# Moving the top-k selection earlier beside the projections, and adding the second softmax map on TensorE, in a two-layer hybrid block

## The chip, the cores and the metric

The kernel runs on 1 core of one Trainium2 chip. One core has TensorE (PE), which multiplies matrices out of SBUF into eight PSUM banks, and VectorE (DVE), ScalarE (ACT) and GpSimd (POOL), which work on tiles of 128 partitions; SyncE (SP) issues the transfers between HBM and SBUF. The metric is the device time of one execution of the whole program, in microseconds (us), lower is better.

## The reference, cut to what matters

The program computes two transformer blocks on a sequence of 1024 tokens of width 1024, batch 1, all in float32. The change lies in the first block's mixer alone: the input projection, the index branch and the two kinds of attention.

```python
h = x @ w_in                       # queries, keys, values of all branches
out_a = gmlp_mixer(a_u, a_v, ...)  # u * (spatial weights @ layer_norm(v))

# differential attention, 4 heads, 2 maps each, 128-query blocks i = 0..7
logits = q[h, m] @ k[h, m].T * scale - slope[h] * |t - s|     (masked)
attn   = softmax(logits[m=0]) - lam * softmax(logits[m=1])
o      = attn @ v[h]               # then rms_norm over the 128 values

# attention on selected keys, 4 heads of 64
score  = sum over 8 index heads of wi * relu(qi @ ki.T)
sel    = the 256 keys of highest score of each query (ties: lowest index first)
p      = softmax(q @ k[sel].T * scale - slope * distance)
o      = p @ v[sel]

x = layer_norm(alpha * x + concat(out_a, out_b, out_c) @ w_out)
```

The feed-forward parts and the second block follow, and the change does not touch them.

## The kernel before, in words

Each engine has a program of its own, written out by hand, and the engines meet only at semaphores. Within an engine the order of instructions is the order in which the Python generators are stepped, so a place where one instruction waits holds back all that stands behind it on that engine.

**Projections.** Weights come in units of 128x1024 float32. SP loads a unit into one of three `raw` buffers, ACT rounds it to the high part `wh` (`act_feed`, L399), POOL subtracts to get the low part `wl` (`pool_feed`, L408), and five such pairs are held. A projection is 24 matmuls (high by high, high by low, low by high). There are 48 projection steps, `s` = 0 to 47: 8 for the gMLP branch ("a", 512 columns wide), 8 for the values of the first attention ("b", 512), 8 for the values of the second ("c", 256), and 24 for queries and keys (two per unit). Their results go through four PSUM banks. For queries and keys ACT writes the high half and `dve_project` (L867) subtracts the low half.

**Beside them.** The list `turns` says how the streams interleave on each of PE, ACT and DVE: 0 is one step of the selection stream, 1 is one projection, 2 is one step of the gMLP's layer norm, 3 is the gMLP product. The selection stream is 20 score units (PE L908, ACT relu L922, DVE sum L934 and L937), then 31 bits, then an end. In a score unit ACT must have emptied the four score banks of the unit before, before PE writes the next.

**The bits.** The 256th highest score of each query is found bit by bit, from the top: for a trial threshold, DVE counts in four of the six query blocks (L964, with the count as a second output), ACT counts in the two widest by summing signs (L956), and small DVE instructions on 6 columns settle the bit and set the next trial. The end is one step that corrects ACT's thresholds by one representable number and counts once more (`dve_next_up`, then L964), and six steps that mark the kept keys of a block (`jk`, a running sum, two comparisons, and the distance bias where a key is kept).

**Attention.** 48 events stand in a fixed order: 8 blocks of head 0 of the first kind ("b"), then b and "c" (second kind, two heads at once) in turn, then 8 b, then b and c in turn. At place `t`, PE runs the logits of event `t` (L1151), the product with the values of event `t - 4` (L1242), and turns the weights of event `t - 2` (L1216, a transpose by the identity). DVE adds the bias and takes the row maximum (L1178), and scales it (L1182). ACT takes the exponential (L1188), copies the turned weights (L1228) and writes the outputs (L1265). For a b event DVE adds the second map to the first (`dve_whole`, L1197, L1199, L1202) before PE turns the sum. On DVE eight places of the attention alternate with the last seven steps of the selection. Logits pass through four banks and the turned weights and outputs through four others.

## Time and profile before

| what | value |
|---|---|
| median of 3 runs | 2943.95 us (2943.65 to 2946.85) |
| the profiled execution | 2947.86 us, of which the span of the core is 2945.7 us |
| busy in the span: PE, DVE, ACT, POOL | 2629.0, 1167.8, 829.2, 622.3 us |
| granted clock of TensorE, mean | 0.945 of full speed |
| first score unit and first projection | from 91.5 us on |
| last projection ends, attention's first logits start | about 396 us |
| last product with values ends | about 657 us |
| the mixed rows are turned for the output projection | from 668.07 us on |

The profile shows one execution. Start times are microseconds from the start of the span. A row of the timeline is one instruction, or several alike merged (xN), with the time from the first's start to the last's end; the bracket says how long the engine had been idle and which instruction released it. Matmuls overlap in the pipeline, so a single matmul lasts longer than the distance from one to the next.

### The profile page before, as it was taken

What the parts mean: (1) busy time and instruction counts of PE and PEld (TensorE: products, weight loads), DVE (VectorE), ACT (ScalarE), POOL (GpSimd) and SP (SyncE); (2) the same over time, 40 slices, a digit from 0 to 9 for tenths busy, and PEclk for the clock granted to TensorE, in tenths of its full rate; (3) what the DMA queues carried; (4) which work ended last, traced back from release to release, by engine and by line L of the source; (5) the groups of instructions that cost most, each with busy time, mean ns of one, the idle gap of its engine ahead of it and who ended that gap; (6) DMA issues with size and microseconds to landing.
All of it is one profiled execution on the core that took longest, in us unless ns stands there. A gap on an engine that the chain in (4) does not pass through costs nothing.

```text
span 2945.7 us, 31283 instructions
## 1 busy us (share of the span) xinstructions
PE 2629.0 (89%) x12551; PEld 2109.2 (72%) x12551; DVE 1167.8 (40%) x2259; ACT 829.2 (28%) x1510; POOL 622.3 (21%) x313
## 2 busy tenths in 40 slices
PE   5999946878898999999994989999859999999998
PEld 4677735767686887887873866666748788788786
DVE  1369998662722323223226015556251111111114
ACT  2345545661311111121112114334231111111022
POOL 1011210001111211221225114447111122222120
PEclk9999978989999999999996999999979999999999
DMA  4013541204023232323411110001231111111122
GB/s 134 22 56 92 181 166 46 84 20 160 8 65 93 86 84 85 97 65 101 129 51 75 47 29 15 15 15 44 72 107 44 43 43 57 48 39 58 36 86 93
DMA packets 195720, 205.45 MB, mean 70 GB/s; under 512 B 13788, under 2 KB 143340, under 8 KB 195576
## 3 DMA queue, kind: packets, MB, share of 16 engines
q1 hardware_dynamic: 195576, 203.46, 21.7%
q8 instruction: 99, 1.62, 0.2%
q14 instruction: 45, 0.37, 0.0%
HBM read 170.88 MB, written 32.56 MB: 69 GB/s over the span
## 4 chain that ended last, share of the span: by engine, by line
PE 71%; DVE 18%; ACT 4%; issue 3%; POOL 2%; DMA 2%; SPq 0%; DVEq 0%; ACTq 0%; POOLq 0%
PE bank L427 12%; PE bank L428 12%; PE bank L429 12%; PE bank L450 8%; PE bank L451 7%; PE bank L452 7%; DVE junk L964 4%; PE bank L1971 2%; PE bank L1242 2%; DVE res L1178 1%; ACT sq L537 1%; PE bank L469 1%; POOL wl L408 1%; PE bank L1151 1%; PE bank L1959 1%
## 5 line engine op out<-in xcount | busy, mean ns | idle before, releaser
L408 POOL TENSOR_TENSOR wl<-raw,wh 128x1024 fp32r<-128x1024 f32 x189 | 452.5, 2412 | 2099.5 <-ACT wh L399 2099.5
L427 PE MATMUL bank<-yh,wh 128*128 128x512 f32 x1536 | 602.1, 392 | 10.1 <-DVE ql L1917 7.2
L429 PE MATMUL bank<-yh,wl 128*128 128x512 f32 x1536 | 598.7, 390 | 0.0
L428 PE MATMUL bank<-yl,wh 128*128 128x512 f32 x1536 | 598.7, 390 | 0.0
L399 ACT ACTIVATE wh<-raw 128x1024 fp32r<-128x1024 f32 x189 | 195.9, 1053 | 613.2 <-PE bank L452 256.3
L427 PEld LDWEIGHTS bank<-yh,wh 128*128 128x128 f32 x1536 | 289.2, 188 | 79.4 <-issue 8.3
L429 PEld LDWEIGHTS bank<-yh,wl 128*128 128x128 f32 x1536 | 288.9, 188 | 60.4
L428 PEld LDWEIGHTS bank<-yl,wh 128*128 128x128 f32 x1536 | 289.1, 188 | 59.5 <-issue 0.2
L1642 DVE TENSOR_TENSOR sil_gate<-sil_gate,bank 128x512 f32<-128x512 f32 x44 | 30.3, 688 | 379.7 <-PE bank L429 379.7
L1662 DVE TENSOR_TENSOR res<-bank,res 128x512 f32<-128x512 f32 x112 | 76.1, 689 | 257.6 <-PE bank L452 257.5
L1642 DVE TENSOR_TENSOR sil_gu<-sil_gu,bank 128x512 f32<-128x512 f32 x44 | 30.3, 688 | 327.0 <-PE bank L429 217.3
L450 PE MATMUL bank<-wh,yh 128*128 128x512 f32 x384 | 154.8, 403 | 2.6 <-DVE yl L2031 1.4
L451 PE MATMUL bank<-wl,yh 128*128 128x512 f32 x384 | 152.4, 397 | 0.0
L452 PE MATMUL bank<-wh,yl 128*128 128x512 f32 x384 | 151.9, 396 | 0.0
L2050 POOL TENSOR_TENSOR took<-took,rest 128x512 f32<-128x512 f32 (+3 forms) x96 | 112.5, 1191 | 89.2 <-DVE rest L2011 50.9
L450 PE MATMUL bank<-wh,hh_gu 128*128 128x512 f32 x256 | 106.9, 418 | 9.0 <-DVE hm_gu L1646 6.7
L964 DVE TENSOR_SCALAR_CACHE_REDUCE junk<-score,cand 128x384 bf16<-128x384 f32 (+3 forms) x132 | 108.9, 825 | 4.7
L450 PE MATMUL bank<-wh,hh_gate 128*128 128x512 f32 x256 | 101.4, 396 | 8.9 <-DVE hm_gate L1646 6.7
L469 PE MATMUL bank<-con,res 128*128 128x128 f32 x192 | 35.3, 342 | 81.5 <-POOL res L1759 31.2
L451 PE MATMUL bank<-wl,hh_gu 128*128 128x512 f32 x256 | 105.1, 410 | 0.0
L452 PE MATMUL bank<-wh,hl_gu 128*128 128x512 f32 x256 | 103.9, 406 | 0.0
L452 PE MATMUL bank<-wh,hl_gate 128*128 128x512 f32 x256 | 100.9, 394 | 0.0
(285 smaller groups left out, 4465.6 us busy)
## 6 DMA issues: line engine op xcount, KB each, us to landing
raw<-in_w_cond SPq DMA_DIRECT2D x48, 512.0 KB, 3.9
raw<-in_w_gu SPq DMA_DIRECT2D x44, 512.0 KB, 5.3
raw<-in_w_down SPq DMA_DIRECT2D x44, 512.0 KB, 3.6
raw<-in_w_in SPq DMA_DIRECT2D x40, 512.0 KB, 4.1
raw<-in_w_gate SPq DMA_DIRECT2D x22, 512.0 KB, 3.9
raw<-in_w_up SPq DMA_DIRECT2D x22, 512.0 KB, 4.0
res<-in_x SPq DMA_DIRECT2D x16, 512.0 KB, 8.4
raw<-in_w_out SPq DMA_DIRECT2D x16, 512.0 KB, 3.7
```

Source lines behind the costliest of these rows:

```text
L399: act.i.activation(wh[n % NU][:, :], raw[u % NRAW][:, :], ACT.Copy).then_inc(*av.up(("wh", u)))
L408: pool.i.tensor_tensor(wl[n % NU][:, :], raw[u % NRAW][:, :], wh[n % NU][:, :].bitcast(F32), ALU.subtract).then_inc(*po.up(("wl", u)))
L427: pe.i.matmul(bank[:, :], a, a_h[:, s], start=k == 0, stop=False)
L428: pe.i.matmul(bank[:, :], a, a_l[:, s], start=False, stop=False)
L429: last = pe.i.matmul(bank[:, :], b, a_h[:, s], start=False, stop=k == 7)
L450: pe.i.matmul(bank[:, 0:wide], xa, h[:, c:c + wide], start=k == 0, stop=False)
L451: pe.i.matmul(bank[:, 0:wide], xa, l[:, c:c + wide], start=False, stop=False)
L452: last = pe.i.matmul(bank[:, 0:wide], xb_, h[:, c:c + wide], start=False, stop=k == nk - 1)
L469: last = pe.i.transpose(bank[:, 128 * k:128 * k + 128], src[:, c:c + 128], idn)
L964: dve.i.tensor_scalar(junk[:, 0:ln], score[:, o:o + ln], 0.0 if thr is None else thr[:, n:n + 1], 0.0, op, ALU.add, accum_out=cnt[:, n:n + ...
L1662: dve.i.tensor_tensor(dst, uses.held[key][:, :], dst, ALU.add).then_inc(*dv.frees(uses, key))
L2050: pool.i.tensor_tensor(s_[:, 0:n], s_[:, 0:n], rest_of[t % 4][:, 1:n + 1], ALU.mult).then_inc(*po.up(("share", t)))
```

## The change

- **Turns.** `FIRST_BITS` goes from 16 to 10. Each of the first ten projection steps now has two score units ahead of it (before: 20 units over 16 steps, so 4 steps had two). Bits stand beside steps 10 to 40, the correcting step beside 41, and the six marking steps beside 42 to 47. The gMLP's norm moves from steps 8 to 15 to steps 2 to 9.
- **Order of projections.** The values of the second kind ("c") go last, steps 40 to 47; queries and keys are steps 16 to 39. The waits on the staging buffers follow.
- **The small steps of a bit.** A bit had four small DVE instructions (a fused one for ACT's signs, compare, exclusive or, exclusive or with the next bit). Now it has three: the counts are taken below the threshold and compared with a column of limits, which also fit ACT's sum of signs; a fused shift and exclusive or; and an exclusive or with a constant out of a table `powers`, which 31 small memsets and a cast write once, early.
- **The end of the selection** uses a free part of `res` for the running sum (`running`), and so waits no longer for the last projections; nothing of it stands inside the attention.
- **The second map.** `dve_whole` goes. DVE writes the identity scaled by the ratio of the two maps (`diag`, 128x128), and PE turns and adds at once: for each 128x128 block one matmul of the first map with the identity and one of the second with `diag`, into the same bank, where there was one transpose.
- **The maximum** is taken as a minimum of logits that are already multiplied by minus the slope, so its separate scaling (L1182) goes.
- **Outputs.** Both maps of a c event share one PSUM bank, and DVE writes them with one multiplication (`dve_outputs`), which stands between the two logits of a place; ACT keeps the b outputs. The reciprocals of both sums are one instruction, one place after the event. SP stores a c block one place later.

On DVE, one bit with its projection reads before (a query and key step; `prl` is the low half of a projection, `cand` holds thresholds and counts):

```order
L964 TENSOR_SCALAR junk,cand<-score,cand 128x384
L964 TENSOR_SCALAR junk,cand<-score,cand 128x512
L964 TENSOR_SCALAR junk,cand<-score,cand 128x640
L964 TENSOR_SCALAR junk,cand<-score,cand 128x768
L1031 SCALAR_TENSOR_TENSOR cand<-cand 128x2
L1034 TENSOR_SCALAR cand<-cand 128x6
L1036 TENSOR_TENSOR cand<-cand 128x6
L1039 TENSOR_SCALAR cand<-cand 128x6
L867 SCALAR_TENSOR_TENSOR prl_84<-bank,prh_82 128x512
```

and now, at the same kind of step:

```order
L981 TENSOR_SCALAR junk,cand<-score,cand 128x384
L981 TENSOR_SCALAR junk,cand<-score,cand 128x512
L981 TENSOR_SCALAR junk,cand<-score,cand 128x640
L981 TENSOR_SCALAR junk,cand<-score,cand 128x768
L1051 TENSOR_TENSOR cand<-cand 128x6
L1053 SCALAR_TENSOR_TENSOR cand<-cand 128x6
L1057 TENSOR_TENSOR cand<-cand,powers 128x6
L884 SCALAR_TENSOR_TENSOR prl_84<-bank,prh_82 128x512
```

The four counts stay, and one of the small instructions behind them is gone.

On DVE, at the third event of the attention, before (L1044 is the last instruction of the correcting step, L1056 and L1058 the first of the marking; `res` holds the weights of the maps):

```order
L1044 TENSOR_SCALAR cand<-cand 128x6
L1178 ISA res,st<-bank,nd 128x256
L1178 ISA st 128x1
L1182 TENSOR_SCALAR st<-st 128x1
L1178 ISA res,st<-bank,nd 128x256
L1178 ISA st 128x1
L1182 TENSOR_SCALAR st<-st 128x1
L1197 RECIPROCAL st<-st 128x1
L1199 SCALAR_TENSOR_TENSOR st<-st,cand 128x1
L1202 SCALAR_TENSOR_TENSOR res<-res,st 128x128
L1056 TENSOR_SCALAR junk<-score,cand 128x384
L1058 SCALAR_TENSOR_TENSOR tcum<-junk 128x384
```

and now, from the last instruction of the marking on:

```order
L1080 SCALAR_TENSOR_TENSOR score<-score,nd 128x1024
L1193 ISA res,st<-bank,nd 128x128
L1193 ISA st 128x1
L1193 ISA res,st<-bank,nd 128x128
L1193 ISA st 128x1
L1193 ISA res,st<-bank,nd 128x256
L1193 ISA st 128x1
L1193 ISA res,st<-bank,nd 128x256
L1193 ISA st 128x1
L1210 RECIPROCAL st<-st 128x2
L1214 SCALAR_TENSOR_TENSOR st<-st,cand 128x1
L1220 TENSOR_SCALAR diag_111<-con,st 128x128
```

All six marking steps now stand ahead of the first logits, and the wide addition of two maps is replaced by one instruction of 128 columns.

On PE, at place 6 (logits of block 6, values of event 2, weights of event 4; `con` is the identity), before:

```order
L1151 MATMUL bank<-kh_88,qh_86 128x384 x2
L1151 MATMUL bank<-kl_89,qh_86 128x384 x2
L1151 MATMUL bank<-kh_88,ql_87 128x384 x2
L1242 MATMUL bank<-v_90,pt_103 128x128 x3
L1216 MATMUL bank<-con,res 128x128 x5
```

and now:

```order
L1168 MATMUL bank<-kh_88,ql_87 128x384 x2
L1265 MATMUL bank<-v_90,pt_103 128x128 x3
L1236 MATMUL bank<-con,res 128x128
L1237 MATMUL bank<-diag_111,res 128x128
L1236 MATMUL bank<-con,res 128x128
L1237 MATMUL bank<-diag_111,res 128x128
```

where the last two rows stand five times in all: ten matmuls in the place of five transposes. The logits and the products with the values are as they were.

The diff, cut to its core:

```diff
-        N_PROJECT, V0, QK0, FIRST_BITS = 48, 8, 24, 16
+        N_PROJECT, V0, QK0, CV0, FIRST_BITS = 48, 8, 16, 40, 10
...
-            turns += [0] * ((20 * (s + 1)) // FIRST_BITS - (20 * s) // FIRST_BITS if s < FIRST_BITS else s < FIRST_BITS + 31) + [1]
-            if V0 <= s < V0 + 8:
+            turns += [0, 0, 1] if s < FIRST_BITS else [0, 1]
+            if 2 <= s < 10:
                 turns.append(2)
...
+        def dve_powers():
+            for b in range(31):
+                dve.i.memset(powers[:, b:b + 1], float(2 ** b)).then_inc(*dv.up())
...
-                dve_count(own, cand[:, 0:6], ALU.is_ge)
+                dve_count(own, cand[:, 0:6], ALU.is_lt)
                 dve.wait_ge(*av.after(("signs", b)))
-                dve.i.scalar_tensor_tensor(out=cnt[:, 4:6], in0=signs, scalar=-0.5, in1=middle, op0=ALU.mult, op1=ALU.add
+                dve.wait_ge(*dv.now())
+                dve.i.tensor_tensor(rj, cnt, limit, ALU.is_gt).then_inc(*dv.up())
+                dve.wait_ge(*dv.now())
+                dve.i.scalar_tensor_tensor(out=cu, in0=rj, scalar=b, in1=cu, op0=ALU.logical_shift_left, op1=ALU.bitwise_xor
                                            ).then_inc(*dv.up())
-                dve.wait_ge(*dv.now())
-                dve.i.tensor_scalar(rj, cnt, 256.0, float(2 ** b), ALU.is_lt, ALU.mult).then_inc(*dv.up())
-                dve.wait_ge(*dv.now())
-                dve.i.tensor_tensor(cu, cu, rj, ALU.bitwise_xor).then_inc(*dv.up())
                 if b:
                     dve.wait_ge(*dv.now())
-                    dve.i.tensor_scalar(cu, cu, 1 << (b - 1), None, ALU.bitwise_xor).then_inc(*dv.up(("threshold", b - 1)))
+                    dve.i.tensor_tensor(cu, cu, bits[:, b - 1:b].broadcast_to([128, 6]), ALU.bitwise_xor
+                                        ).then_inc(*dv.up(("threshold", b - 1)))
...
             dve.wait_ge(*nd_in.after("nd"))
-            dve.wait_ge(*mm.after(("project", N_PROJECT - 1)))
...
-                                           scale=1.0, scalar=mx[:, 0:1] if z else -3.0e38, op0=ALU.add, op1=ALU.max,
+                                           scale=-slope_of(t, m), scalar=mx[:, 0:1] if z else 3.0e38, op0=ALU.add, op1=ALU.min,
...
+        def dve_sums(t):
+            sums, rc = small((t, "sums"), 2), small((t, "rc"), 2)
             dve.wait_ge(*av.after((t, 1, "exp")))
...
+            dve.i.reciprocal(rc, sums).then_inc(*dv.up((t, "rc")))
+            if events[t][0] == "b":
...
+                dve.i.tensor_scalar(diag[u % 2][:, :], idn, c2, None, ALU.mult).then_inc(*dv.up((t, "diag")))
...
-                    last = pe.i.transpose(bank[:, 128 * b:128 * b + 128], vb[:, 128 * (c0 + b):128 * (c0 + b) + 128], idn)
+                    if kind == "b":
+                        pe.i.matmul(o, va[:, s], idn, start=True, stop=False)
+                        last = pe.i.matmul(o, vb[:, s], diag[place_b[t] % 2][:, :], start=False, stop=True)
+                    else:
+                        last = pe.i.transpose(o, va[:, s], idn)
...
+        def dve_outputs(t):
...
+            dve.wait_ge(*mm.after((t, 1, "out")))
+            dve.wait_ge(*osc_out[i % 4].after(("c", g, i - 4) if i >= 4 else ("c", g - 1, i + 4)))
+            dve.i.tensor_tensor(osc[:, 128 * (i % 4):128 * (i % 4) + 128].rearrange("p (m c) -> p m c", m=2),
...
                 if t < N_EVENT:
                     dve_logits(t, 0)
+                u = lagging(t, 4, "c")
+                if u is not None:
+                    dve_outputs(u)
+                if t < N_EVENT:
                     dve_logits(t, 1)
-                u = lagging(t, 1, "b")
-                if u is not None:
-                    dve_whole(u)
-                u = lagging(t, 4)
+                u = lagging(t, 1)
                 if u is not None:
                     dve_sums(u)
...
-            attend = dve_attend()
-            step(order(8, 7), attend, selection)
-            rest(attend, selection)
+            dve_attend()
```

## Rows read from the trace of the kernel before

**Rows 1.** Windows: stretch, its length, busy PE, PEld, DVE, ACT, POOL, clock.

```profile
400.00:450.00 50.00, 12.21 (x52) 8.27 (x52) 46.88 (x123) 13.59 (x32) 3.50 (x2) 0.55 0.44 152
```

**Rows 2.** Timeline of PE, place 8 of the attention: start, length, instruction, idle before.

```profile
473.45 0.47 PE L1151 MATMUL bank<-kh,qh 64*128 64x128 f32 x2 [6.12 <-DVE st L1178]
```

**Rows 3.** Timeline of DVE and POOL: bits alone, then a bit beside weight splits.

```profile
253.61 0.61 DVE L964 TENSOR_SCALAR_CACHE_REDUCE junk<-score,cand 128x384 bf16<-128x384 f32 x1
...
257.73 0.61 DVE L964 TENSOR_SCALAR_CACHE_REDUCE junk<-score,cand 128x384 bf16<-128x384 f32 x1
...
282.33 0.15 DVE L1031 SCALAR_TENSOR_TENSOR cand<-cand 128x2 f32<-128x2 f32 x1
282.41 2.39 POOL L408 TENSOR_TENSOR wl<-raw,wh 128x1024 fp32r<-128x1024 f32 x1 [8.16 <-ACT wh L399]
282.52 2.31 DVE L1034 TENSOR_SCALAR cand<-cand 128x6 uint32<-128x6 f32 x1
...
294.07 2.31 DVE L1034 TENSOR_SCALAR cand<-cand 128x6 uint32<-128x6 f32 x1
```

**Rows 4.** Timeline of PE: starts of score units, one step with one, one with two.

```profile
104.83 0.51 PE L908 MATMUL bank<-ikh,iqh 32*128 32x512 f32 x4
...
111.64 0.51 PE L908 MATMUL bank<-ikh,iqh 32*128 32x512 f32 x4
...
115.09 0.80 PE L908 MATMUL bank<-ikh,iqh 32*128 32x512 f32 x4 [2.24 <-ACT res L922]
...
123.38 0.51 PE L908 MATMUL bank<-ikh,iqh 32*128 32x512 f32 x4
```

**Rows 5.** Timeline of POOL and ACT: weights split at the end of the b values.

```profile
216.17 7.42 POOL L408 TENSOR_TENSOR wl<-raw,wh 128x1024 fp32r<-128x1024 f32 x3 [53.86 <-ACT wh L399]
...
222.91 1.06 ACT L399 ACTIVATE wh<-raw 128x1024 fp32r<-128x1024 f32 x1 [4.15 <-DMA raw<-in_w_in]
```

**Rows 6.** Timeline of DVE: correcting step, narrowest and widest marking step.

```profile
407.76 0.29 DVE L974 TENSOR_SCALAR cand<-cand 128x2 uint32<-128x2 uint32 x1
...
420.56 0.17 DVE L1044 TENSOR_SCALAR cand<-cand 128x6 f32<-128x6 f32 x1
...
422.63 0.42 DVE L1056 TENSOR_SCALAR junk<-score,cand 128x384 bf16<-128x384 f32 x1
...
425.38 0.56 DVE L1065 SCALAR_TENSOR_TENSOR score<-score,nd 128x384 f32<-128x384 f32 x1
...
464.01 0.75 DVE L1056 TENSOR_SCALAR junk<-score,cand 128x1024 bf16<-128x1024 f32 x1
...
469.77 1.23 DVE L1065 SCALAR_TENSOR_TENSOR score<-score,nd 128x1024 f32<-128x1024 f32 x1
```

**Rows 7.** Groups by form of PE, 473 to 657: count, busy, mean ns, idle before.

```profile
L1242 PE MATMUL bank<-v,pt 128*128 128x128 f32 x268 | 42.4, 311 | 7.8 <-ACT osc L1265 7.7
L1216 PE MATMUL bank<-con,res 128*128 128x128 f32 x267 | 42.0, 296 | 12.5 <-ACT osc L1265 10.1 <-ACT osb L1265 2.3
L1242 PE MATMUL bank<-v,pt 128*128 128x64 f32 x288 | 36.2, 281 | 0.0
```

**Rows 8.** Timeline of PE at full clock: eight transposes, eight blocks of values.

```profile
479.47 1.04 PE L1216 MATMUL bank<-con,res 128*128 128x128 f32 x8
...
483.41 2.05 PE L1242 MATMUL bank<-v,pt 128*128 128x128 f32 x16
```

**Rows 9.** Windows: all places from 8 on, and the steadiest stretch in them (PE only).

```profile
473.00:657.00 184.00, 156.86 (x1183) 133.76 (x1183) 130.43 (x506) 129.85 (x324) 0.00 (x0) 0.91 0.17 58
...
500.00:537.00 37.00, 30.83 (x261) 1.00 0.03 9
```

**Rows 10.** Timeline of ACT and DVE: from the last product with values on.

```profile
656.95 0.31 ACT L1265 ACTIVATE osc<-bank,st 128x64 f32<-128x64 f32 x1 [1.48 <-PE bank L1242]
657.28 1.28 ACT L1282 ACT_TABLE_LOAD   x1
...
659.27 2.19 DVE L1294 SCALAR_TENSOR_TENSOR osb<-osb,st,sg 128x128 f32<-128x128 f32 x8
```

More of the change, by code:

```diff
@@ L1 @@
-from itertools import repeat
+from itertools import chain, repeat
 from contextlib import ExitStack
@@ L258, in build @@
         tcum, osb, osc = sb("tcum", 1024), [sb(f"osb{i}", 1024) for i in range(2)], sb("osc", 512)
-        junk, junk_a = sb("junk", 1024, BF, 512), sb("junk_a", 1024, BF, 512)
-        sg = sb("sg", 128)
+        junk = sb("junk", 1024, BF, 512)
+        diag = [sb(f"diag{i}", 128) for i in range(2)]
+        area(place[0] - 256)
+        junk_a = sb("junk_a", 1024, BF, 512)
+        sg, powers = sb("sg", 128), sb("powers", 32)
+        running = res[:, 7168:8192]
         area(low)
@@ L794, in project_steps @@
                         yield n, m, half
+            for tb in range(8):
+                yield "c", tb, None
         projects = list(project_steps())
@@ L1378, in sp_mix @@
         def sp_mix():
-            sp.wait_ge(*av.after((place_of["c", 1, 7], 1, "out")))
+            sp.wait_ge(*dv.after((place_of["c", 1, 7], "out")))
             for tb in range(8):
@@ L2261, in act_program @@
             act_lambda()
-            selection = (x for part in (act_scores(), act_topk()) for x in part)
+            selection = chain(act_scores(), act_topk(), repeat(None))
             step(turns, selection, act_project(), act_gmlp_norm(), repeat(None))
-            rest(selection)
             act_attend()
@@ L2279, in dve_program @@
             dve_weights()
-            selection = (x for part in (dve_scores(), dve_topk()) for x in part)
-            step(turns, selection, dve_project(), dve_gmlp_norm(), once(dve_gmlp))
-            attend = dve_attend()
-            step(order(8, 7), attend, selection)
-            rest(attend, selection)
+            step(turns, chain(dve_scores(), dve_topk()), dve_project(), dve_gmlp_norm(), once(dve_gmlp))
+            dve_attend()
             dve_mix()
```

130 lines of the change are left out of this document (64 added, 66 removed).

## The prediction

> **What bounds the kernel now.** I read the page first: PE is busy 89% of the span and carries 71% of the chain of waits, DVE 18%. So a change pays where PE idles or runs at the low clock. The windows then show the place: from 400 to 450 PE is busy 12.2 of 50 us, DVE 46.9, and the granted clock is 0.55 [rows 1]. DVE is finishing the bits and the end of the selection there, between the first places of the attention, and PE waits for its logits to be read. Place 8, the first of the second head, starts at 473.45 after one more such wait [rows 2]. From place 8 on the picture is another one: PE is busy 156.9 of 184 us, DVE 130.4, ACT 129.9, and in the steadiest stretch PE is busy 30.8 of 37 at clock 1.00 [rows 9]. There PE is the bound or close to it. The change takes from DVE in both parts and gives to PE in the second, so I sum four stages: the scores, the bits to the end of the selection, the first eight places, the places from 8 on.
>
> **Scores.** A step with one score unit takes 111.64 - 104.83 = 6.81 us, of which the projection is about 5.5; one with two takes 123.38 - 111.64 = 11.74 [rows 4]. The second unit costs 4.93 where one alone costs 1.3, since PE waits 2.24 for ACT to empty the banks and then runs slowly for a while. Six more steps have two units: 6 x 3.6 = 22; four of the ten pairs are narrower than 512 columns and cheaper, so I take 19 (12 to 25). Before, the b values ended at about 219: their weights are freed and the next ones split from 216.17 on [rows 5]. Now they end at 219 + 19 + 3.4 for the gMLP product, which moves into this stretch (an estimate: four float32 matmuls of 512 columns, so eight records at about twice the 0.23 of a projection's 5.5 / 24): 241. The first ten steps end at 241 - 3.4 - 6 x 5.5 = 204.6.
>
> **Bits.** One bit alone takes 257.73 - 253.61 = 4.12 [rows 3]. One of its four small instructions goes, 0.2 us at most; but the first of them no longer starts under the last count, so I take 0.07 (0 to 0.2): 4.05. DVE starts the selection's own part at 204.6 + 3 for the last piece of the norm, spends 6 on the first six counts (about the second half of the correcting step [rows 6]), six bits at 4.05 and 2.7 on the gMLP product (an estimate: four instructions of 512 columns, at half of 1.23 for 1024 [rows 6] and a little more): 240.6. At the end of the b values POOL splits four units, 7.42 us for three and then one more [rows 5]. Before, that met an idle DVE; now it meets bits. A small instruction that meets a split lasts 2.31 instead of 0.17 [rows 3], and three in a row would be met: 7 us (0 to 9.5), 247.6. ACT also waits there for the fourth unit's transfer, 4.15 us [rows 5], with the next bit's signs queued behind it on ACT and DVE waiting for those: step 16 ends at about 252.4. Then every second step meets one split: 294.07 - 282.52 = 11.55 for two bits with two projections [rows 3], less 0.14, is 5.7 each. 23 steps: 131 us, 383.5. PE needs 5.5 per step and runs ahead by up to four banks, so DVE sets this pace and PE does not stop. Step 40: 4.05 + 2.3, 389.9. The correcting step takes 420.73 - 407.76 = 13.0 [rows 6]: 402.9. The six marking steps take 3.3 us for the narrowest and 7.0 for the widest [rows 6], evenly between, 6 x 5.15 = 30.9: 433.8. Two units for the output projection are split under them, and nearly every instruction of the marking can be met: 4.7 (0 to 5). The selection ends at 438.5. PE has ended its projections at about 397, since those of the c values are half as wide and need DVE only for the last banks; it then idles some 40 us, less the logits that fit in four banks.
>
> In sentences that the sum does not need: the Trainium skill, SBUF — State Buffer, section "SBUF: two separate sides" with "Who interferes with whom", says that a DVE instruction with two SBUF inputs contends with a GpSimd instruction that reads SBUF, and that a tensor-scalar form can contend through its two-port mode. The blocked row here is a tensor-scalar [rows 3]; the three new small instructions all have two inputs. By that rule the stall stays and the sum is as above; if only the old form were blocked, 2.3 us would go at every second step, the second rival below.
>
> **First eight places.** PE needs, at full clock, 21 blocks turned at four passes each (10.4), 10 blocks of values (2.5) and logits (an estimate, 72 records at the 0.09 of below, 6.5): 19.4. DVE's reading of the same logits I estimate at 20; it is the slower one in the small blocks and PE in the large, so the larger of the two sum to some 22. PE comes out of a long idle time, at half clock, so I take 26 (22 to 32). Place 8 starts at 464.5, 9 us earlier than at 473.45 [rows 2].
>
> **Places from 8 on.** Sixteen records of the values' matmul take 2.05 and eight transposes 1.04 [rows 8], overlap apart 0.124 and 0.121 each at full clock. The 556 records of the values are 69 us, the 267 transposes 32 [rows 7], the other 360 of the 1183 [rows 9], logits, at 0.09 about 32: 133 us of PE at full clock in 184. Each b block now has two matmuls in float32, each of which shows two records (16 for eight blocks [rows 8]), so four records for one. From place 8 on 4 x 36 - 21 = 123 b blocks are turned: 369 more records, 45.8 us. PE's work becomes 179. What remains of the 51 us above the work, 27 idle and 24 of low clock? The waits for ACT to free an output bank, 10.1 + 7.7 [rows 7], mostly go, since c events use one bank instead of two and DVE frees it early. The halts while ACT loads the square root's table stay, and so does some low clock behind them. Also a c event needs all four banks while ACT is copying. I take 19 (5 to 31): 198, so 14 us more (0 to 26). DVE loses 81 scalings and the wide additions, some 25 of its 130 us, and gains 32 narrow ones and the c outputs; at about 110 beside 179 it is no bound any more, and its relief is worth nothing here.
>
> **The end.** After the last product ACT writes the output, loads the table, and DVE ends at 661.46, 4.5 us after 656.95 [rows 10]. The square and the sum over 1024 columns of the last head stood on DVE under that product; now DVE writes the last c output ahead of them. Each is like the widest marking instruction, 1.23 [rows 6], and a small one 0.17: 2.7 more (2 to 3.5).
>
> **At nothing.** 31 memsets and a cast at 0.17 or less are 5 us on DVE, ahead of the index branch, in slices where the page shows DVE one to three tenths busy; cover gone, 5. SP stores a c block a place later, with several places before anybody reads it. The heads' loads start after the last projection at 397, before they are needed at 464.
>
> **Sum.** -9 + 14 + 2.7 = 7.7 more. Against the profiled execution, 2947.86, that is 2955.6. That execution is 3.9 above the median of the runs, so I predict 2951.
>
> **Rivals.**
> 1. TensorE stays at its high clock. Before, clock 0.91 over places 8 on [rows 9] went with idle gaps; denser work leaves fewer. Then the 24 us of low clock go as well as most waits: 184 again from place 8, and -9 + 0 + 2.7 gives 2937.5. For it: 1.00 where gaps are 2 us [rows 9]. Against: the table halts stay, and PE must keep up with a work that is a third larger. The Trainium skill, TensorE: Matmul & The Clock Gate, "Part 4: PE-mode transpose", says that a transpose does not count as PE being busy for the clock; by that rule matmuls in its place help this rival, while the stretch at 1.00 had transposes all along.
> 2. The collisions with POOL go or move. Then the query and key steps run at PE's 5.5, the selection ends some 11 us earlier, and the sum is -3.3: 2940.5. Against: ACT's split starts a fixed time after the threshold, and so do the small instructions; the pair 282.41, 282.52 repeats 11.55 later [rows 3].
> 3. The gains and the loss cancel: the selection ends near 431, or PE pays 6 rather than 14: 2944, no change. It differs from the forecast by sizes alone.
> 4. The coupling through the four banks. DVE now waits for the product of a c event before it reads the second logits, and ACT's four copies free the banks that the next output needs. At 0.8 us for each of 16 c places, 12 more: 2963. It decides if a c place exceeds PE's own work by more than 0.7.
>
> **How the numbers follow.** The forecast (sum between +2 and +15, 2946 to 2959) has 0.42; rival 1 0.20, rival 2 0.12, rival 3 0.14, rival 4 0.12. About 0.2%, 5.9 us, can be told from no change. Faster: 0.14 of rival 1, 0.06 of rival 2, 0.04 of the rest, 0.24. Within: 0.12 of the forecast, 0.06 + 0.06 + 0.10 of rivals 1 to 3, 0.34. Slower: 0.28 of the forecast, 0.12 of rival 4, 0.02, 0.42. The range, 2934 to 2965, reaches over rivals 1 and 4.
>
> **What would show it.** In the changed kernel's timeline: steps of 11 to 12 us in all of the first ten; the second half of the bits with one small instruction of 2.3 us at every second step; no small instruction of four; the first logits read at 438 (428 to 448); place 8 at 464; from there to the last product 198 us at a clock above 0.91, with PE busy over 90%; DVE's square of the last head behind the last product. I am wrong if place 8 starts before 455, if the places from 8 on take under 190 us, or if the records of the b blocks are fewer than four each.

## The result: slower by 0.34%, and the profile after

| | before | changed |
|---|---|---|
| median of 7 runs each, in turn on one chip | 2946.7 us (2942.73 to 2947.11) | 2955.09 us (2950.9 to 2960.77) |
| ratio, 95% interval | | 1.0034 (1.0022 to 1.0046) |
| profiled execution, span | 2947.86, 2945.7 us | 2960.77, 2959.0 us |

The forecast was 2951 (2934 to 2965), most likely slower. Both spans can be cut at the same events: first score unit on PE, first small DVE instruction behind the six counts that open the bits, first running sum of the marking, PE's start on places 8 and 47 of the attention, first turn of the mixed rows. I use these cuts for every kernel below. Each row below comes from one profiled execution of each kernel, so a difference of a few us in the scores or in the rest can be chance.

| stage, us | before | changed |
|---|---|---|
| up to the first score unit | 91.5 | 93.2 |
| scores | 142.6 | 124.0 |
| bits and correction | 189.0 | 194.0 |
| marking and first eight places | 50.4 | 54.1 |
| places 8 to 47 | 163.2 | 176.6 |
| place 47 to the first turn | 31.4 | 37.7 |
| the rest | 2277.6 | 2279.4 |

So the selection brings place 8 forward by 8.1 us, and the attention behind it gives back 19.6.

Windows of the changed kernel, the two that answer to [rows 1] and to the first of [rows 9], then the steadiest stretch with all engines (columns as there):

```profile
400.00:450.00 50.00, 14.56 (x101) 12.29 (x99) 45.88 (x72) 9.56 (x24) 4.66 (x2) 0.62 0.38 134
465.00:667.00 202.00, 189.06 (x1556) 170.43 (x1554) 100.95 (x385) 121.74 (x291) 0.00 (x0) 0.97 0.16 53
500.00:537.00 37.00, 34.60 (x297) 30.99 (x296) 21.35 (x80) 22.60 (x48) 0.00 (x0) 1.00 0.03 9
```

PE is busy 94% of the 202 us and DVE half of them: the work really moved, onto the engine that was already the bound. The first window looks as before, since PE still waits there for DVE, only for a different reason. These are the rows around the end of the marking; the third is PE's first one after it:

```profile
440.59 1.22 DVE L1080 SCALAR_TENSOR_TENSOR score<-score,nd 128x1024 f32<-128x1024 f32 x1
441.74 0.28 DVE L1193 CUSTOM_DVE_ANT_0 res<-bank,nd 128x128 f32<-128x128 f32 x1
442.38 0.69 PE L1168 MATMUL bank<-kh,qh 64*128 64x384 f32 x2 [35.38 <-DVE st L1193]
...
465.31 0.33 PE L1168 MATMUL bank<-kh,qh 64*128 64x128 f32 x2
```

All of DVE's work for the selection now stands in one piece ahead of the attention, and PE's wait for it is 35.38 us long. Place 8 starts at 465.31, which answers to [rows 2].

The groups of PE by form from 465 to 667, which answer to [rows 7]:

```profile
L1236 PE MATMUL bank<-con,res 128*128 128x128 f32 x248 | 50.1, 285 | 2.4 <-DVE diag L1220 2.4
L1237 PE MATMUL bank<-diag,res 128*128 128x128 f32 x248 | 49.4, 282 | 0.0
L1265 PE MATMUL bank<-v,pt 128*128 128x128 f32 x268 | 40.3, 301 | 5.4 <-ACT pt L1251 5.4
L1265 PE MATMUL bank<-v,pt 128*128 128x64 f32 x288 | 35.3, 277 | 0.0
L1239 PE MATMUL bank<-con,res 128*128 128x128 f32 x144 | 18.9, 274 | 2.2 <-ACT osb L1279 2.2
```

The 267 transposes of before are 144 (c events), and the b blocks have 248 + 248 records: 124 blocks at four, where I had counted 123. The waits for ACT's `osc`, 17.8 us before, are gone.

The bits, at the same place as [rows 3]:

```profile
282.39 2.39 POOL L412 TENSOR_TENSOR wl<-raw,wh 128x1024 fp32r<-128x1024 f32 x1 [9.14 <-ACT wh L403]
282.51 2.30 DVE L1051 TENSOR_TENSOR cand<-cand 128x6 uint32<-128x6 f32 x1
284.84 0.17 DVE L1053 SCALAR_TENSOR_TENSOR cand<-cand 128x6 uint32<-128x6 uint32 x1
285.04 0.17 DVE L1057 TENSOR_TENSOR cand<-cand,powers 128x6 uint32<-128x6 uint32 x1
...
288.22 1.01 DVE L981 TENSOR_SCALAR_CACHE_REDUCE junk<-score,cand 128x768 bf16<-128x768 f32 x1
289.34 0.17 DVE L1051 TENSOR_TENSOR cand<-cand 128x6 uint32<-128x6 f32 x1
```

One instruction in every second step still lasts 2.3. Two bits take 11.54 us (294.05 - 282.51) where [rows 3] have 11.55. The last two lines show why the instruction saved is worth almost nothing even where nobody collides. Before, the instruction that combined ACT's signs did not need DVE's last count and ran in the 1.12 us from the start of that count to the compare. Now the compare starts 289.34 - 288.22 = 1.12 after it as well.

At the end of the b values [rows 5] two small instructions in a row were met by POOL's splits. The correcting step and the marking begin at the rows that follow them; they answer to [rows 6]:

```profile
244.46 2.27 DVE L1053 SCALAR_TENSOR_TENSOR cand<-cand 128x6 uint32<-128x6 uint32 x1
246.76 2.32 DVE L1057 TENSOR_TENSOR cand<-cand,powers 128x6 uint32<-128x6 uint32 x1
...
393.83 0.17 DVE L991 TENSOR_SCALAR cand<-cand 128x2 uint32<-128x2 uint32 x1
...
406.50 2.21 DVE L1063 TENSOR_SCALAR cand<-cand 128x6 f32<-128x6 f32 x1
408.81 2.38 DVE L1071 TENSOR_SCALAR junk<-score,cand 128x384 bf16<-128x384 f32 x1
```

The last two are stretched as well, by 4.0 us together: the two splits for the output projection fall there.

The end of the attention, DVE, which answers to [rows 10]:

```profile
667.09 0.29 DVE L1289 TENSOR_TENSOR osc<-bank,st 128x128 f32<-128x128 f32 x1 [6.77 <-PE bank L1265]
667.48 1.23 DVE L1298 TENSOR_TENSOR tcum<-osb 128x1024 f32<-128x1024 f32 x1
```

The square of the last head stands behind the last product, as forecast: DVE waited 6.77 us for it with the square queued behind.

The score stage, PE's unit starts, and what held one of them up, which answers to [rows 4]:

```profile
169.40 0.45 PE L925 MATMUL bank<-ikh,iqh 32*128 32x384 f32 x4
180.27 0.51 PE L925 MATMUL bank<-ikh,iqh 32*128 32x512 f32 x4
...
184.47 1.06 ACT L403 ACTIVATE wh<-raw 128x1024 fp32r<-128x1024 f32 x1 [4.33 <-DMA raw<-in_w_in]
...
187.50 2.04 ACT L939 ACTIVATE res<-bank 128x512 f32<-128x512 f32 x4
189.68 0.80 PE L925 MATMUL bank<-ikh,iqh 32*128 32x512 f32 x4 [8.20 <-ACT res L939]
```

At the end of the gMLP's values ACT waits for a weight transfer, with four copies of scores queued behind it, and PE's second unit waits for those. That transfer wait was there before too (2.96 us), on a step with a single unit, where no second unit was held up.

### The profile page after: what moved, and what is told of

Same layout as the page of the kernel before. It is cut to its first block, busy times and chain, and to the rows that moved or that the text cites. A ratio compares the mean times of both kernels' runs of the same rounds, so it can differ in the third digit from the quotient of the medians.

```text
span 2959.0 us, 31957 instructions
## 1 busy us (share of the span) xinstructions
PE 2664.5 (90%) x12983; PEld 2155.5 (73%) x12983; DVE 1139.1 (38%) x2136; ACT 825.8 (28%) x1482; POOL 620.5 (21%) x313
## 4 chain that ended last, share of the span: by engine, by line
PE 72%; DVE 16%; ACT 5%; issue 3%; POOL 2%; DMA 2%; SPq 0%; DVEq 0%; ACTq 0%; POOLq 0%
PE bank L431 12%; PE bank L432 12%; PE bank L433 12%; PE bank L454 7%; PE bank L455 7%; PE bank L456 7%; DVE junk L981 4%; PE bank L1265 2%; PE bank L1996 2%; ACT sq L541 1%; PE bank L1168 1%; PE bank L473 1%; POOL wl L412 1%; DVE cand L1051 1%; PE bank L1984 1%
## 5 line engine op out<-in xcount | busy, mean ns | idle before, releaser
L456 PE MATMUL bank<-wh,yl 128*128 128x512 f32 x384 | 153.0, 399 | 0.0
L455 PE MATMUL bank<-wl,hh_gate 128*128 128x512 f32 x256 | 100.9, 394 | 0.0
```

The source lines that it names most:

```text
L455: pe.i.matmul(bank[:, 0:wide], xa, l[:, c:c + wide], start=False, stop=False)
L456: last = pe.i.matmul(bank[:, 0:wide], xb_, h[:, c:c + wide], start=False, stop=k == nk - 1)
```

## Experiments

Every kernel was timed against the kernel before on the same chip; the medians of the kernel before lie between 2945.9 and 2946.7 us, so the medians of different experiments can be compared to about 1 us as far as the chips go. Medians of 4 to 12 runs of one kernel still move by a few us. The changed kernel has three separable parts in the attention (who adds the maps; who writes the c outputs; scalings, shared bank and reciprocals) and one outside.

**1. DVE adds the maps again.** In `dve_sums` and `pe_over`:

```diff
-                dve.i.tensor_scalar(diag[u % 2][:, :], idn, c2, None, ALU.mult).then_inc(*dv.up((t, "diag")))
+                dve.i.scalar_tensor_tensor(out=a[:, 0:ln], in0=b[:, 0:ln], scalar=c2, in1=a[:, 0:ln], op0=ALU.mult,
+                                           op1=ALU.add).then_inc(*dv.up((t, "whole")))
...
-                    if kind == "b":
+                    if kind == "b" and pe_maps(t):
```

> The changed kernel, with one thing undone: in b events DVE adds the second map to the first with one wide instruction, as before the change, and TensorE turns the sum by transposes, one record per block instead of four. Narrow scalings gone, c outputs on DVE and the whole selection stay as changed. Theory A (the loss is the 46 us of float32 matmuls that TensorE got for the b blocks where it is the bound): places 8 on fall from 201.7 to 184 us or less, the first eight places grow by 0 to 4 us since DVE limits them, and the whole is 2941 us (2936 to 2946) against 2955 of the changed kernel. Rival B (the loss comes from the c outputs on DVE and the one bank they share): places 8 on stay at 198 to 202 us and the whole at 2952 to 2957.

Measured: 2930.53 us, ratio to before 0.9952 (0.994 to 0.9964). That is 24.6 below the changed kernel, where theory A said 14: right in kind, too small in size. Places 8 to 47 take 153.0 us, the marking with the first eight places 50.5 instead of 54.1, the stretch from place 47 to the first turn 35.0 instead of 37.7. These three sum to 29.8 us in the profiles, the medians say 24.6.

**2. The kernel before, with the maps on TensorE alone.** The same edit the other way round.

> The kernel before, with one part of the change alone: TensorE adds the second map of b events through a scaled identity (two float32 matmuls per block for one transpose), DVE makes the scaled identity instead of the wide addition. Selection, projections, scalings and outputs stay as before. Theory A: the first eight places gain up to 3 us, since DVE is relieved where it is the bound, and places 8 on grow from 183.5 by 14 to 20 us; the whole is 2946.7 + 11 to 20, so 2961. Rival B: TensorE's added work fills its own idle time, the whole stays within 4 us of 2946.7.

Measured: 2969.42 us, 1.0082 (1.0069 to 1.0095): 23.4 more than before. Places 8 to 47 take 186.5 instead of 163.2, and PE's clock is 0.94 where [rows 9] have 0.91. Theory A again, and again more than I expected. The price of the maps between places 8 and 47 is the same in both settings: 186.48 - 163.24 = 23.2 here, 176.55 - 153.04 = 23.5 in the first experiment. In the first head it is not: here the stretch from the first running sum to place 8 takes 48.0 us instead of 50.4, so where DVE does the marking between the first places, TensorE's adding gains 2.4 us, as theory A had it.

**3. The selection alone**, with the whole attention as before.

> The changed kernel with its whole attention as before (narrow scalings, DVE adds the maps, ACT writes the c outputs in two banks); order of the projections, three-step bits and the end of the selection as changed. Theory A: the selection ends at about 442 as in the changed kernel, place 8 starts at 465 to 468, places 8 on take 184 and the end is as before: 2946.7 - 6 to 9, so 2939 us (2936 to 2942). Rival B (the earlier selection is given back because projections and loads stand later): 2945 to 2950.

Measured: 2936.71 us (12 runs), 0.9973 (0.9964 to 0.9983): 9.3 less than before. In its profile, of an execution 9.7 us above the median, place 8 starts at 466.86, and places 8 to 47 take 164.6, 1.4 more than before. The selection's part does what it should, and the attention behind it gives little of that back.

**4. TensorE adds the maps in the first head only**, `pe_maps(t)` being `t < 8`.

> The changed kernel, but TensorE adds the maps only in the first eight places, where it waits for DVE after the selection; from place 8 on DVE adds them as before the change. Theory A: place 8 starts at 465 as in the changed kernel, places 8 on take 184 us or less, the whole is 2937 us (2933 to 2943), up to 4 us under the kernel in which DVE adds them all. Rival B: 2952 to 2957, as the changed kernel. Rival C (TensorE limits the first eight places too): 1 to 3 us above the kernel in which DVE adds them all.

Measured: 2935.22 us, 0.9962 (0.9951 to 0.9974), some 5 above the first experiment's: rival C. The marking with the first eight places takes 54.1 instead of 50.5, and places 8 to 24 take 63.1 instead of 59.6, since the events of places 6 and 7 are turned at places 8 and 9. With the maps on it PE limits the first head too: in the changed kernel it is busy 22.9 of the 23.0 us from its first row after the marking to place 8, at a mean clock of 0.85, and DVE 16.8. DVE's relief there is worth nothing once the whole marking stands ahead.

**5. c outputs back on ACT**, on top of the first: two copies of 64 columns out of the shared bank.

```diff
-                u = lagging(t, 4, "b")
+                u = lagging(t, 4)
                 if u is not None:
                     act_outputs(u)
...
-                u = lagging(t, 4, "c")
-                if u is not None:
-                    dve_outputs(u)
```

> The kernel in which DVE adds the maps (2930.5 us), with the c outputs given back to ACT: two copies of 64 columns out of the one shared bank, where DVE wrote both with one instruction; the narrow scalings stay gone. It tells which part of the attention's edits brought the 11.6 us between places 8 and 47 (153.0 us against 164.6 with the attention as before). Theory A (TensorE waited for ACT to free output banks, 17.8 us in the kernel before, and DVE's early write ends that): the 11.6 us mostly come back, the whole is 2937 to 2942 us. Rival B (the one bank for two outputs, or the missing scalings on DVE, brought it): within 3 us of 2930.5.

Measured: 2922.04 us, 0.9917 (0.9904 to 0.993). Both expectations fall: it is 8.5 *faster*. I ran this kernel and the first once more, side by side:

> The kernel in which DVE adds the maps, run once more beside the next, on one chip: its profile showed the score stage 8.7 us longer than the other's, with the same code there. Theory A (in this stage an execution draws drops of the granted clock, whatever the kernel's attention): the median again 2928 to 2934, the score stage anywhere from 210.8 to 219.5 at its end, and places 8 to 47 again 153 us. Rival B (the code's own place or length makes it): the stage ends at 219 again.

> The same with the c outputs on ACT. Theory A: the median 3 to 9 us below the kernel beside it, 2922 to 2928; the difference within the attention is about 3.4 to 7 us, places 24 to 31 take 33.6 us against 40.5, the score stage ends anywhere from 210.8 to 219.5. Rival B: the stage ends at 211 again.

Measured: 2928.8 us, 0.9938 (0.9926 to 0.995), and 2919.53 us, 0.991 (0.9897 to 0.9924): 9.3 apart. Theory A holds in kind: the score stage of the kernel with DVE's outputs ended at 219.5 the first time and at 213.6 now, with the same code, and the difference within the attention came back, while 2919.53 and the 9.3 lie just outside its ranges. Places 24 to 32 take 40.5 and 33.6 us in all four profiles. The stretch from place 47 to the first turn takes 35.0 and 30.4. Here is what the DVE outputs do at places 23 to 29, in the repeat of the first (DVE and PE; `osc` is the c output):

```profile
516.35 0.29 DVE L1301 TENSOR_TENSOR osc<-bank,st 128x128 f32<-128x128 f32 x1 [1.92 <-PE bank L1277]
...
528.02 0.29 DVE L1301 TENSOR_TENSOR osc<-bank,st 128x128 f32<-128x128 f32 x1 [2.83 <-PE bank L1277]
...
537.19 0.29 DVE L1301 TENSOR_TENSOR osc<-bank,st 128x128 f32<-128x128 f32 x1 [3.02 <-PE bank L1277]
...
539.18 1.23 DVE L1310 TENSOR_TENSOR tcum<-osb 128x1024 f32<-128x1024 f32 x1
540.44 1.22 DVE L1312 TENSOR_REDUCE st<-tcum 128x8 f32<-128x1024 f32 x1
...
543.73 0.80 PE L1171 MATMUL bank<-kh,qh 64*128 64x512 f32 x2 [4.05 <-DVE st L1199]
```

and in the repeat with the outputs on ACT:

```profile
514.48 0.50 ACT L1295 ACTIVATE osc<-bank,st 128x64 f32<-128x64 f32 x2
...
522.63 0.52 ACT L1295 ACTIVATE osc<-bank,st 128x64 f32<-128x64 f32 x2 [1.79 <-PE bank L1277]
...
531.80 0.52 ACT L1295 ACTIVATE osc<-bank,st 128x64 f32<-128x64 f32 x2 [1.55 <-PE bank L1277]
...
534.95 0.50 PE L1171 MATMUL bank<-kh,qh 64*128 64x512 f32 x2 [1.12 <-DVE st L1199]
```

In the first, DVE stands up to 3 us before an output, with logits, the wide addition and the square and sum of a finished head (539.18, 540.44) queued behind, and PE then waits for its logits to be read (4.05 at place 29, where it waits 1.12 with the outputs on ACT). With the outputs on ACT, DVE does the square and sum while PE is at the product. Place by place, the two repeats differ at places 24 and 28 above all, 3.0 and 3.3 us; the outputs on ACT cost about 1 us each at places 14 and 38. This is the first half of my rival 4, DVE waiting for a c event's product.

**6. The changed kernel with c outputs back on ACT.** The edit is that of experiment 5.

> The changed kernel, with the c outputs alone given back to ACT (two copies from the shared bank); TensorE still adds the maps. Theory A (DVE, waiting for the product of a c event ahead of its second logits, holds TensorE's banks at the pass from the mixed heads to the next, places 24 to 28, whoever adds the maps): 5 to 9 us less than the changed kernel's 2955, so 2946 to 2950, the gain within places 24 to 31. Rival B (with the maps on TensorE it is the bound and its work alone counts): within 2 us of 2955.

Measured: 2953.32 us (11 runs), 1.0022 (1.0013 to 1.0031): 1.8 below the changed kernel by the medians. Places 24 to 32 do gain 5.8 us, as theory A says, but places 8 to 47 take 176.8, as before the edit, because two other places lose as much: 14 and 38, 2.9 us each, 7.19 instead of 4.33. There PE waits for a bank. These are its rows and ACT's at place 14, then those of the changed kernel:

```profile
489.61 0.49 ACT L1283 ACTIVATE osc<-bank,st 128x64 f32<-128x64 f32 x2
490.25 0.77 PE L1236 MATMUL bank<-con,res 128*128 128x128 f32 x2 [2.75 <-DVE osb L1331]
```

```profile
486.45 0.28 DVE L1289 TENSOR_TENSOR osc<-bank,st 128x128 f32<-128x128 f32 x1
487.92 0.49 PE L1236 MATMUL bank<-con,res 128*128 128x128 f32 x2 [1.19 <-DVE diag L1220]
```

The bank that PE turns event 12 into is the one that held the output of event 9. With ACT as writer it comes free at 490.10, behind two table loads for the square root of the finished head and two exponentials; the row names a DVE instruction that ended about then, but nothing of PE's there depends on that. With DVE as writer it was free at 486.73 (place 14 starts at 485.89 here and at 485.12 there). The rows after the wait also run slower (0.77 instead of 0.49). So DVE's outputs help beside the table loads and hurt beside the product of a long c event, and between places 8 and 47 the two cancel here. Only the end keeps its 4.6 us: 3.3 before the last product, 1.3 behind it. Up to the first turn and without the score stage the profiles differ by 5.8 us, the medians by 1.8, so between rival B (within 2) and theory A (5 to 9) the whole time does not decide. Rival 4's mechanism costs less here than with the maps on DVE.

**7. ACT splits ahead of the signs**, in the changed kernel, so that POOL works under DVE's counts. A split then starts 0.33 us behind the first count of its bit (283.98, 283.65) instead of 3.37 (282.39, 279.02):

```diff
-                act_feed(project_released(s))
+                if half is not None and s < CV0 - 1:
+                    held_back.append(project_released(s))
+                else:
+                    act_feed(project_released(s))
...
             for b in BITS:
+                if held_back:
+                    act.wait_ge(*dv.after(("threshold", b)))
+                    act_feed(held_back[-1])
+                    held_back.clear()
```

> The changed kernel, where in the query and key steps ACT splits the next weights ahead of the next bit's signs (behind the same threshold) instead of behind the projection's copy, so that GpSimd's difference falls under DVE's counts and not on its small instructions. Theory A (the collision sets the pace of the bits): no small instruction of 2.3 us in these steps, two steps take TensorE's 11.0 to 11.1 us instead of 11.54, the selection ends 5 to 7 us earlier, about 2949 us against 2955. Rival B (the signs, 1.1 us later, end behind the counts and hold the small instructions): two steps take 11.4 to 11.6 us, the whole within 2 us of 2955. Rival C (the counts, one-input instructions, are blocked too): steps of 11.5 or more.

Measured: 2942.89 us (12 runs), 0.9988 (0.9976 to 0.9999): 12.2 below the changed kernel, twice what I expected. Theory A; the rows:

```profile
283.98 2.41 POOL L412 TENSOR_TENSOR wl<-raw,wh 128x1024 fp32r<-128x1024 f32 x1 [7.26 <-ACT wh L403]
...
284.30 0.75 DVE L990 TENSOR_SCALAR_CACHE_REDUCE junk<-score,cand 128x512 bf16<-128x512 f32 x1
285.09 0.88 DVE L990 TENSOR_SCALAR_CACHE_REDUCE junk<-score,cand 128x640 bf16<-128x640 f32 x1
...
287.14 0.17 DVE L1060 TENSOR_TENSOR cand<-cand 128x6 uint32<-128x6 f32 x1
```

The counts under POOL's 2.41 us keep their 0.75 and 0.88, and the small instruction is back to 0.17. Bits and correction take 176.4 us instead of 194.0. The sum I had in mind left out that PE had run ahead: until about 284 two bits take 9.41 us (264.91 - 255.50 between splits), and only then TensorE's 10.88 (294.86 - 283.98).

**8. DVE adds the maps, and ACT splits ahead.**

> Both: DVE adds the second maps, and ACT splits ahead of the signs. Theory A: 2930.5 - 5 to 7, so 2924 us. Rivals B and C: 2929 to 2932.

Measured: 2914.74 us, 0.9895 (0.988 to 0.9909), 15.8 below the first experiment's. Again A, and more.

**9. All three edits together.**

> All three together: DVE adds the maps, c outputs as two ACT copies from the shared bank, ACT splits ahead of the signs. If the gains are independent: 2922.0 - 15.8 = 2906 us (2902 to 2912), place 8 at 445 to 447, places 8 to 47 in 148 us. Rival: the earlier selection only exposes ACT, which now has the outputs too; 2912 to 2917, no better than without the outputs moved.

Measured: 2906.77 us (2897.81 to 2908.87), 0.9862 (0.9846 to 0.9877), the best version found: the gains add, as far as 4 runs tell. Of the 17.6 us of the bits, about 4 come back in the marking, where two splits now fall at 400.50:

```profile
400.50 5.11 POOL L412 TENSOR_TENSOR wl<-raw,wh 128x1024 fp32r<-128x1024 f32 x2 [19.10 <-ACT wh L403]
400.65 2.77 DVE L1084 SCALAR_TENSOR_TENSOR junk<-res,cand,junk 128x512 bf16<-128x512 f32 x1
403.45 2.71 DVE L1087 SCALAR_TENSOR_TENSOR score<-score,cand,junk 128x512 f32<-128x512 f32 x1
```

The same two instructions take 0.75 each in the changed kernel.

**10. Bits from the fourteenth projection**, on top of all three: `FIRST_BITS` 14, six steps with two score units instead of ten.

> The kernel with all three edits (2906.8 us), with the score units spread over 14 projections instead of 10 (six steps with two units instead of ten), so that the bits start four steps later and the last four pieces of the marking come behind the projections. It prices the change's 'from the tenth projection on'. Theory A (each step with two units costs 3.6 us more than one with a single unit, and four projections of 5.5 go in front of the bits): the bits start 22 - 14 = 8 us later (130 to 137 us after the first score matmul, against 119.5 to 127), the selection ends 6 to 9 us later, the whole is 2912 to 2916 us. Rival B (the doubled units leave TensorE gaps in which the clock falls, and four fewer pay for the later start): within 2 us of 2906.8 or less.

Measured: 2910.68 us (2907.61 to 2913.55), 0.9875 (0.9858 to 0.9891): 3.9 more, between the two expectations. The intervals of the two ratios overlap (0.9846 to 0.9877 beside 0.9858 to 0.9891). In the profiles the mixed rows are first turned at 628.60 us here and at 628.25 in the ninth experiment, and the difference lies behind, in code that is the same (2282.0 and 2278.6). Scores and bits take 2.1 us more each, the stretch from the marking to place 8 takes 4.0 less (50.8 instead of 54.8): the splits no longer meet the marking. So "tenth rather than fourteenth" is worth little here, if anything.

## Why the prediction was right, step by step

The forecast and its sign were right: up to the first turn the profiles differ by 11.5 us, where the sum had 7.7, and the medians by 8.4. The sum gave 2951.7 rather than 2951, and its base, 2943.95 from 3 runs, was 2.75 below the median of 7. The steps:

- **Scores.** Predicted end of the first ten steps 204.6; the last unit starts at 201.48, and the projection behind it ends at about 208.2, 3.6 us late. I had counted steps of 11 to 12 throughout, but those with narrow units take down to 7.9, and the held-up one (180.27 to 198.04) 17.8. Nearly right in sum, by two errors that offset, which is luck.
- **Bits.** From the first small instruction behind the opening counts to the correcting step I had 213.6 to 389.9, 176.3 us, and the trace has 217.24 to 393.83, 176.6: the 3.6 us of delay came in with the scores. The pace of 5.7 per step held (11.54 for two); the 0.07 for the fourth small instruction was 0.02. At the end of the b values two small instructions were met, not three (2.27 and 2.32). The 252.4 for the end of step 16 holds some 0.6 us that the sum gives no source for. The two splits for the output projection met one small instruction of the correcting step and one of the marking, 4.0 us, where 4.7 was forecast. The first logits are read at 441.74, not 438.5, within the 428 to 448 that I named.
- **First eight places.** Place 8 at 465.31; forecast 464.5. From the first logits read that is 23.6 us, where I had taken 26: this error made up for most of the delay.
- **Places 8 on.** Forecast 198 us to the last product, so 14 more; measured 667.05 - 465.31 = 201.7, so 18 more. The records are as forecast. The +14 was 45.8 of work against 32 of slack. Between places 8 and 47, 13.3 more were measured, and the experiments take them apart: 23.5 for the maps, and some -10 for scalings, bank, reciprocals and outputs together (experiment 2 and the changed kernel, both with the maps on TensorE, 186.5 - 176.6 = 9.9; with the outputs on ACT in both, experiments 2 and 6, 186.5 - 176.8 = 9.7). The slack absorbs somewhat less than half of the added work: for these places it is 115 blocks x 3 records x 0.124 = 42.8 us, of which 23.5 are paid. Of the 19.3 absorbed, 7.6 were idle time of PE (18.5 us in experiment 1, 10.9 in the changed kernel), and the rest goes with a clock of 0.97 instead of 0.91. Whether DVE's relief is "worth nothing here", as I wrote, no run tells: the narrow scalings were never undone by themselves.
- **The end.** Forecast 2.7 more; from the last product to the first turn it is 679.55 - 667.05 = 12.5 against 11.2 before, so 1.3 more, and the same 1.3 stands between all profiles with the c outputs on DVE (12.4 to 12.6) and on ACT (11.0 to 11.3). What I did not see is that these outputs also cost 3.3 us ahead of the last product (22.5 instead of 19.2 from place 47 on, with the maps on DVE).
- **At nothing.** The table `powers` costs nothing that shows: the first score unit starts at 90.8 to 93.2 us in the kernels that write it and at 91.5 and 92.4 in the two that do not.
- **Rival 1** is half true: the clock rose from 0.91 to 0.97 [rows 9], and the work took all of it. The Trainium skill, TensorE: Matmul & The Clock Gate, "Part 4: PE-mode transpose", says that a transpose does not count as PE being busy in the same way; by that, matmuls in its place should help the clock. The traces agree in direction (0.91 with transposes in experiment 1, 0.97 with matmuls), but the matmul version also idles less, so no run here separates the two. Between places 8 and 47 the clock goes with PE's idle time also among kernels whose transposes are the same (0.89 at 26.0 us of idle time in experiment 3, 0.91 at 18.5 in experiment 1, 0.93 at 16.7 in experiment 5), which speaks for idle time.
- **Rival 2** did not happen by itself, and experiment 7 shows what it would have brought: 12.2 us, where I had taken 11 (a sum of -3.3 for one of 7.7).
- **Rival 3** asked for a selection that ends near 431 or a price of 6 us on PE; neither came.
- **Rival 4** is in part a real mechanism: DVE's wait for a c event's product. The c outputs on DVE cost 8.5 and 9.3 us in all with the maps on DVE, and 1.8 (by the profiles 5.8) in the changed kernel, where they also save 2.9 at each of two places. The 12 us more that I gave it did not come.

By medians, on one path from before to the changed kernel (experiments 3, 5, 1): selection -9.3, scalings with bank and reciprocals -14.7, c outputs to DVE +8.5, maps to TensorE +24.6. That the four sum to +9.1, beside the 8.4 measured directly, is no check, since each step starts where the last one ended; and their sizes hold for this order, as the c outputs show. Experiments 3 and 5 differ by scalings, shared bank and reciprocals, and by SP's store of a c block one place later; they are 14.7 apart, 17.2 with the repeat.

Open: what scalings, bank and reciprocals are worth apart. No run separates them, but the traces lean. Here are PE's waits between places 8 and 47 in experiment 3, then in the repeat of experiment 5 (total, times, longest):

```profile
PE bank L1233 <- ACT osc L1284: 8.7, 5, 2.0
PE bank L1259 <- ACT osc L1284: 7.7, 4, 3.3
PE bank L1168 <- DVE st L1195: 6.9, 6, 2.5
PE bank L1233 <- ACT osb L1284: 3.5, 4, 1.2
```

```profile
PE bank L1251 <- ACT osc L1295: 9.5, 7, 3.1
PE bank L1171 <- DVE st L1199: 6.0, 4, 3.6
```

Waits for a bank that ACT empties for `osc` fall from 16.4 to 9.5 us, waits for logits that DVE reads only from 6.9 to 6.0. And in experiment 3 ACT's outputs themselves waited 7.1 us, 19 times, for reciprocals, which DVE wrote behind the logits of the same place; written three places earlier they are never waited for in experiment 5. So the bank and the earlier reciprocals are likelier than the missing scalings.

## What to carry to other kernels

Before work moves from one engine to another, ask which engine is the bound in each stage where it runs: here the addition of the maps was moved to relieve DVE, and in the changed kernel TensorE paid for it in every stage, the first head included. In the kernel before, where DVE was the bound of the first head, the same move gained 2.4 us there and lost 23.2 behind. A bundle that comes out near zero may hold large parts of both signs, so cut the spans at the same events and undo one part at a time. An instruction that waits for a late result belongs on the engine that nobody needs just then, and that can differ from place to place. And when one short instruction in a serial chain is stretched by elementwise work on a neighbour engine, moving that work by some 3 us can be worth far more than shortening the chain: 12 to 16 us here, against 0.02 per bit for the instruction saved.

## What was not expected of the hardware

The score stage takes 119.5 to 127.0 us in kernels whose code is the same there. The same kernel (experiment 1) shows 126.7 in one profile and 122.3 in another, and experiment 9, with 127.0, differs in its attention and ACT's feed alone. The windows of experiment 1 and of the repeat of experiment 5, at the same time:

```profile
102.00:112.00 10.00, 7.76 (x47) 5.43 (x46) 4.46 (x7) 4.79 (x10) 0.00 (x0) 0.74 0.01 2
```

```profile
102.00:112.00 10.00, 7.77 (x57) 5.70 (x56) 5.86 (x9) 4.79 (x10) 0.00 (x0) 1.00 0.01 2
```

PE is equally busy, and the windows lie within 1.4 us of the same point of the stage, but the granted clock is 1.00 in one, the upper of its two levels (2.4 GHz), and in the other 0.74, a mean over both (1.2 and 2.4 GHz), and 47 matmuls against 57 get done. Over the whole stage it is 0.93 where the stage takes 119.5 us and 0.87 where it takes 127.0. Whether a step with gaps runs at the high or the low clock thus differs between executions. That moves single profiles by up to 7.5 us, more than some of the edits are worth; the medians carry the verdicts here for that reason.

DVE instructions with two SBUF inputs and six columns wait for POOL's whole two-input instruction (0.17 becomes 2.30), while the counts, with one SBUF input, do not. The Trainium skill, SBUF — State Buffer, "SBUF: two separate sides" with "Who interferes with whom", says as much of two-input instructions, and the trace agrees. Of the tensor-scalar form it says that it can contend, except the form that also writes out its accumulator. The traces agree with both: the small ones were held up (2.31 in [rows 3], 2.21 for L1063 now), and so was the plain wide one (L1071, 384 columns, 2.38 instead of the 0.42 of [rows 6]), but the counts, the form with an accumulator, were not.
